# The forgetting attention goes first, with the other attention's preparation laid between its units

## The reference

```
proj = u @ w_in                      # c_q 256, c_kv 128, k_pe 32, fox q/k/v 3*512, f_logit 8
q = rms_norm(rms_norm(c_q) @ w_uq)   # MLA: 8 heads of 96; the last 32 rotated by position
kv = rms_norm(c_kv) @ w_ukv          # 64 key numbers and 64 values a head
k = rms_norm(concat(k_nope, k_pe))   # k_pe is the same 32 numbers for all heads; rotated
o_mla = attention(q, k, v, 96 ** -0.5)
fq, fk = rms_norm(fox_q), rms_norm(fox_k)           # FoX: 8 heads of 64
cum = cumsum(log_sigmoid(f_logit + b_forget))
o_fox = attention(fq, fk, fv, 64 ** -0.5, cum)      # adds cum[t] - cum[s] to the scores
return concat(o_mla, o_fox) @ w_out
```

## Time and profile before

| | |
|---|---|
| median of 3 runs (lowest, highest) | 1681.85 us (1679.6, 1686.58) |
| profiled execution, its own time | 1693.18 us |
| its span, first to last instruction | 1691.4 us |
| mean granted TensorE clock | 0.949 |
| busy: TensorE, VectorE, ScalarE, GpSimd | 91%, 61%, 32%, 33% |
| chain that ended last | TensorE 69%, DMA 20%, VectorE 6%, ScalarE 2% |
| DMA, mean over the span | 338 GB/s |

### The profile page before, as it was taken

How to read it: one execution, slowest core, us unless ns; L and a number is a source line. 1 busy time by engine, 2 the same in 40 slices (tenths; PEclk the granted TensorE clock), 3 DMA queues, 4 the chain that set the end, 5 groups by cost and what they waited for, 6 DMA issues and landing times.

```text
span 1691.4 us, 22760 instructions
## 1 busy us (share of the span) xinstructions
PE 1530.7 (91%) x8260; PEld 1172.0 (69%) x8260; DVE 1024.1 (61%) x2113; ACT 534.0 (32%) x1077; POOL 558.2 (33%) x361
## 2 busy tenths in 40 slices
PE   6999989999999999999999998978887778688877
PEld 6999988678899999998889986534433333233332
DVE  4554355555343325998974845757676776758556
ACT  4433353343344435443115422212121212121213
POOL 3555344000144342001001413444544445353441
PEclk9999999799899998998999999999998989898999
DMA  6767699977889997998976828899999999999995
GB/s 247 254 225 253 235 348 386 322 249 261 299 314 367 371 371 276 363 368 303 324 260 237 321 81 370 321 426 426 427 427 427 427 427 428 426 427 427 427 427 248
DMA packets 98724, 571.87 MB, mean 338 GB/s; under 512 B 10960, under 2 KB 11088, under 8 KB 48976
## 3 DMA queue, kind: packets, MB, share of 16 engines
q1 hardware_dynamic: 60768, 298.41, 48.5%
q0 software_dynamic: 36864, 268.45, 37.8%
q10 hardware_dynamic: 1008, 3.90, 0.6%
HBM read 569.68 MB, written 135.27 MB: 417 GB/s over the span
## 4 chain that ended last, share of the span: by engine, by line
PE 69%; DMA 20%; DVE 6%; issue 2%; ACT 2%; POOL 1%; another core or an unknown queue 0%; ACTq 0%; POOLq 0%; DVEq 0%
DMA arena<-pairs,eidx 18%; PE ps L2213 10%; PE ps L1669 9%; PE ps L1670 9%; PE ps L1671 9%; PE ps L2014 5%; PE ps L2183 2%; PE ps L1720 2%; PE ps L1722 2%; PE ps L1721 2%; DMA ring<-pairs,eidx 2%; PE ps L2031 2%; PE ps L1965 2%; DVE arena L1565 1%; PE ps L1684 1%
## 5 line engine op out<-in xcount | busy, mean ns | idle before, releaser
L2213 PE MATMUL ps<-arena 128*128 128x512 f32 x872 | 420.6, 634 | 90.2 <-ACT arena L1025 90.1
L2213 PEld LDWEIGHTS ps<-arena 128*128 128x128 f32 x872 | 173.0, 203 | 324.6 <-issue 201.9
L1565 DVE CUSTOM_DVE_ANT_0 arena<-arena 128x1024 f32<-128x1024 f32 x218 | 265.4, 1223 | 166.1 <-DMA arena<-pairs,eidx 165.9
L654 POOL TENSOR_TENSOR w_lo<-ring,w_hi 128x1024 fp32r<-128x1024 f32 x82 | 219.0, 2672 | 430.0 <-DVE w_lo L1095 350.3
L684 POOL DMA_INDIRECT arena<-pairs,eidx x218 | 253.6, 1163 | 297.9 <-PE ps L2213 240.1
L1669 PE MATMUL ps<-u_hi,w_hi 128*128 128x256 f32 (+1 forms) x1056 | 305.9, 290 | 10.9 <-DVE u_lo L1064 10.9
L1671 PE MATMUL ps<-u_hi,w_lo 128*128 128x256 f32 (+1 forms) x1056 | 304.2, 288 | 0.0
L1670 PE MATMUL ps<-u_lo,w_hi 128*128 128x256 f32 (+1 forms) x1056 | 303.9, 288 | 0.0
L701 ACT ACTIVATE w_hi<-ring 128x1024 fp32r<-128x1024 f32 x188 | 198.0, 1056 | 170.4 <-PE ps L1722 77.5
L1669 PEld LDWEIGHTS ps<-u_hi,w_hi 128*128 128x128 f32 x1056 | 202.7, 192 | 13.1 <-issue 11.7
L1671 PEld LDWEIGHTS ps<-u_hi,w_lo 128*128 128x128 f32 x1056 | 203.2, 192 | 0.0
(11 more groups left out here) (305 smaller groups left out, 2329.1 us busy)
## 6 DMA issues: line engine op xcount, KB each, us to landing
ring<-in_stream SPq DMA_DIRECT2D x130, 1024.0 KB, 6.7
pairs<-in_peer_u SPq DMA_DIRECT2D x128, 512.0 KB, 7.4
pairs<-in_peer_v SPq DMA_DIRECT2D x128, 512.0 KB, 8.5
arena<-in_ada SPq DMA_DIRECT2D x32, 768.0 KB, 6.3
arena<-pairs,eidx POOLq DMA_INDIRECT x218, 17.2
h<-in_x_t SPq DMA_DIRECT2D x1, 1088.0 KB, 7.4
arena<-in_keys ACTq DMA_DIRECT2D x1, 1024.0 KB, 6.4
out<-arena SPq DMA_DIRECT2D x2, 512.0 KB, 5.2
```

Of the source, the lines that this page charges most:

```text
L654: pool.tensor_tensor(lo[:, half, :], ring[:, slot, e * HALF:(e + 1) * HALF], hi[:, half, :], ALU.subtract).then_inc(used if e else lo_done, 1)
L1565: dve.tensor_tensor_reduce(row, row, hf[:, n % HEAD_ROWS // TOPK, :], 1.0, 0.0, ALU.mult, ALU.add, dots[:, n % HEAD_ROWS:n % HEAD_ROWS + 1 ...
L2213: mm = pe.matmul(ps[:, Y_BANKS[j // TOPK] + half, :], diag[:, n % DIAGS, :], slot_of(n)[:, D + half * 512:D + half * 512 + 512], start=(hd ...
```

## The change

FoX's units get the numbers 0 to 15, MLA's 16 to 31 (`head_of`). Stage 3 is cut up and laid into iterations of the FoX units; all its products go through one bank (7), the squares through bank 2, so that FoX's scores have two banks instead of three. In the FoX loop TensorE turns unit n first, then computes the scores of n+2. A preparation product waits until the bank is read. The turned probabilities get a buffer of their own. The key part that all heads share is rotated once, from one copy, and then copied to the eight heads. The forget gate's Exp and Ln go ahead of the raw keys' evictions. The preparation by iteration:

| iteration | TensorE | VectorE | ScalarE |
|---|---|---|---|
| 0 to 3 | query rotation; 16 squares (0, 1 queries; 2, 3 keys) | three `rope` operations | |
| 4 | shared key's rotation; last squares | rotation, copy to eight heads | |
| 5 to 7 | values of a token tile | 7: inverses of the roots | 6: roots; 7 to 9: value copies |
| 8 to 15 | spread of a key's scale | product with it | |

```diff
@@ scalar
+            act.wait_ge(z_done, 3)
+            act.activation(logf[fr, 1, :], logf[fr, 1, :], ACT.Exp, scale=-1.0).then_inc(f_exp, 1)
+            act.wait_ge(f_exp, 1)
+            act.activation(logf[fr, 2, :], logf[fr, 1, :], ACT.Ln, bias=1.0).then_inc(f_ln, 1)
             for hd in range(HEADS):
                 act.wait_ge(k_raw_mm, hd + 1)
...
                 if n >= 3:
                     head_out(n - 3)
+                if n == ROOT_AT:
+                    key_roots()
+                if ROOT_AT < n <= ROOT_AT + 3:
+                    values(n - ROOT_AT - 1)
@@ vector
-            dve.tensor_scalar(km[pr, :, :], pe_all, V("g_k")[pr], None, ALU.mult).then_inc(kpe_done, 1)
+            dve.tensor_scalar(km[pr, 0, :], praw[pr, 3, :], V("g_k")[pr], None, ALU.mult).then_inc(kpe_done, 1)
...
+            def key_turned():
+
+                shared = pe_sq[pr, :]
+                dve.wait_ge(krot_mm, 1)
+                dve.wait_ge(rope_step, 12)
+                dve.tensor_tensor(turned[pr, 0, :], ps[pr, SPARE_BANK, 0:T], C("sin")[pr, :], ALU.mult).then_inc(rope_step, 1)
+                dve.tensor_tensor(shared, km[pr, 0, :], C("cos")[pr, :], ALU.mult).then_inc(rope_step, 1)
+                dve.wait_ge(rope_step, 14)
+                dve.tensor_tensor(shared, shared, turned[pr, 0, :], ALU.add).then_inc(rope_step, 1)
+                dve.wait_ge(rope_step, 15)
+                dve.tensor_copy(km[pr, :, :], shared[:, None, :].broadcast_to([ROPE, HEADS, T])).then_inc(rope_step, 1)
...
             for n in range(units):
                 if n + 1 < units:
                     soft_max(n + 1)
                 scale_p(n)
+                if n < 4:
+                    query_turned(n)
+                elif n == 4:
+                    key_turned()
+                elif n == ROOT_AT + 1:
+                    key_scales()
+                if KEYS_FROM <= n < KEYS_FROM + HEADS:
+                    key_scaled(n - KEYS_FROM)
                 if n % 2 and n >= units // 2:
                     ada_add(KT // 2 + n // 8, n // 2 % ADA_Q)
@@ tensor
             pe.wait_ge(fstat_sqrt, 2)
+            pe.wait_ge(q_raw_ev, 4)
+            pe.wait_ge(k_raw_ev, HEADS)
             pe.wait_ge(kpe_done, 2)
+            pe.wait_ge(fox_done, 12)
...
+            def values_of(t):
+
+                at, n = token_tiles(0, 3)[t]
+                if t:
+                    pe.wait_ge(vm_ev, t)
+                else:
+                    pe.wait_ge(rope_step, 13)
+                pe.matmul(ps[0:n, SPARE_BANK, :], ckvn[:, at:at + n], wuv, start=True, stop=True).then_inc(vm_mm, 1)
...
             def key_norm(hd):
 
-                if hd >= 4:
-                    pe.wait_ge(kn_done, hd - 3)
+                if hd:
+                    pe.wait_ge(kn_done, hd)
+                else:
+                    pe.wait_ge(mrec2, 1)
+                    pe.wait_ge(vm_ev, 3)
...
             def scores_of(n):
...
-                if n >= 3:
+                if n > FOX_UNITS:
                     pe.wait_ge(exp_done, n - 2)
+                elif n == FOX_UNITS:
+                    pe.wait_ge(mstat_sqrt, 2)
+                elif n >= 2:
+                    pe.wait_ge(exp_done, n - 1)
...
             scores_of(0)
             scores_of(1)
-            for n in range(units):
+            for n in range(FOX_UNITS):
+                turn_probs(n)
+                scores_of(n + 2)
+                if n < 4:
+                    query_rotated(n)
+                elif n == 4:
+                    key_rotated()
+                if n < TT:
+                    query_squares(n)
+                elif n < TT + 3:
+                    key_squares(n - TT)
+                if VALUES_FROM <= n < VALUES_FROM + 3:
+                    values_of(n - VALUES_FROM)
+                if KEYS_FROM <= n < KEYS_FROM + HEADS:
+                    key_norm(n - KEYS_FROM)
+                if n:
+                    weigh(n - 1)
+            for n in range(FOX_UNITS, units):
                 if n + 2 < units:
                     scores_of(n + 2)
                 turn_probs(n)
-                if n:
-                    weigh(n - 1)
+                weigh(n - 1)
```

More of the change, by code:

```diff
@@ L528, in w_parts, with head_of, score_bank @@
             return (late_hi, late_lo, late_hi_f) if part == 2 else (w_hi, w_lo, w_hi_f)
+        UNITS = 2 * HEADS * TT
+        FOX_UNITS = HEADS * TT
+        VALUES_FROM = 5
+        ROOT_AT = 6
+        KEYS_FROM = 8
+        SPARE_BANK = 7
+        STAT_BANK = 2
+        def head_of(n):
+            return (n // TT + HEADS) % (2 * HEADS)
+        def score_bank(n):
+            return n % 2 if n < FOX_UNITS else (n - FOX_UNITS + 2) % 3
         def q_scale(hd, t):
@@ L820, in _, with key_roots, values @@
                 act.activation(ksq[0:NOPE, hd, :], src, ACT.Square).then_inc(k_raw_ev, 1)
[L821 to L826, removed]
-                n = P if t < 2 else N_META
-                act.activation(vM[0:n, t, :], ps[0:n, t, :], ACT.Copy).then_inc(vm_ev, 1)
-            fr = slice(FL_ROW, FL_ROW + HEADS)
-            act.wait_ge(z_done, 3)
-            act.activation(logf[fr, 1, :], logf[fr, 1, :], ACT.Exp, scale=-1.0).then_inc(f_exp, 1)
-            act.wait_ge(f_exp, 1)
-            act.activation(logf[fr, 2, :], logf[fr, 1, :], ACT.Ln, bias=1.0).then_inc(f_ln, 1)
-            units = 2 * HEADS * TT
+            def key_roots():
+                act.wait_ge(mstat_mm, 1)
+                act.activation(mrms[:, 0:32], ps[:, STAT_BANK, 0:32], ACT.Sqrt, bias=eps[:, :]).then_inc(mstat_sqrt, 1)
+                act.activation(mrms[0:N_META, 32:40], ps[0:N_META, STAT_BANK, 32:40], ACT.Sqrt, bias=eps[0:N_META, :]
+                               ).then_inc(mstat_sqrt, 1)
+            def values(t):
+                n = P if t < 2 else N_META
+                act.wait_ge(vm_mm, t + 1)
+                act.activation(vM[0:n, t, :], ps[0:n, SPARE_BANK, :], ACT.Copy).then_inc(vm_ev, 1)
+            units = UNITS
             for n in range(units):
-                hd, t = divmod(n, TT)
+                hd, t = head_of(n), n % TT
                 keys_n = X0 + P * (t + 1)
@@ L1211, in rope, with query_turned @@
                 dve.tensor_tensor(x, x, tmp, ALU.add).then_inc(rope_step, 1)
-            for b in range(4):
+            def query_turned(b):
                 dve.wait_ge(qrot_mm, b + 1)
-                rope(qm[0:QK, 2 * b:2 * b + 2, :], ps[0:QK, HEAD_BANKS[b], :].rearrange("p (a t) -> p a t", a=2),
+                rope(qm[0:QK, 2 * b:2 * b + 2, :], ps[0:QK, SPARE_BANK, :].rearrange("p (a t) -> p a t", a=2),
                      slice(X0, T), b)
[L1217 to L1224, removed]
@@ L1849, in _ @@
                 mla_key(4 + j)
[L1851 to L1859, removed]
@@ new lines, in key_rotated, with query_squares, key_squares @@
+            def key_rotated():
+                pe.wait_ge(rope_step, 10)
+                pe.matmul(ps[0:QK, SPARE_BANK, 0:T], C("rot")[0:QK, 0:QK], km[0:QK, 0, :], start=True, stop=True).then_inc(krot_mm, 1)
+            def query_squares(s):
+                at, n = token_tiles(0, 2)[s]
+                for hd in range(HEADS):
+                    pe.matmul(ps[0:n, STAT_BANK, s * 8 + hd:s * 8 + hd + 1], qsq[0:QK, hd, at:at + n], one, start=True, stop=True)
+            def key_squares(s):
+                at, n = token_tiles(0, 3)[s]
@@ L1891, in _ @@
-            mm.then_inc(vm_mm, 1)
-            for hd in range(4, HEADS):
-                key_rotated(hd)
-            pe.wait_ge(mrec2, 1)
-            pe.wait_ge(vm_ev, 3)
-            for hd in range(HEADS):
-                key_norm(hd)
-            pe.wait_ge(kn_done, HEADS)
-            units = 2 * HEADS * TT
+            units = UNITS
             def scores_of(n):
-                hd, t = divmod(n, TT)
+                hd, t = head_of(n), n % TT
                 keys_n = X0 + P * (t + 1)
```

58 lines of the change are left out of this document (32 added, 26 removed).

## The result

The changed kernel took 1706.98 us (median of six, 1697.39 to 1717.84), the kernel before 1684.21 beside it (1678.82 to 1692.83); the ratio is 1.0116, with a 95% interval of 1.0086 to 1.0147. On the median of 1681.85 known before that is +19.5 us, to 1701. The profiled execution took 1708.26 us against 1693.18.

The account below looks back on a forecast made before the run. Units looked close to TensorE's own work; laid-in preparation would close a TensorE-VectorE ring. Stage end 5.9 us later plus 4 us of clock loss gave +9.9 us on the 1681.85 median: 1692 us, range 1677 to 1703.

Parts of the forecast that it names:

- the first two mechanisms: FoX units: a ring of waits between TensorE and VectorE, and one short clock loss, +4 us.
- the clock's 4 us: Units 0 to 4: one rotation unit at half clock, +4 us, within bounds of 0 and 20.
- Start: Before the first unit: forget gate ahead of ScalarE's key evictions, first scores at 310.5 us, first turning at 314.6.
- The ring: FoX units: turning, scores, product, VectorE's preparation and unit work follow one another; 73.2 us against TensorE's own 60.3.
- The clock in units 0 to 4: Squares and idling in FoX units 0 to 4 put one unit at half clock, +4 us.
- The table loads: ScalarE's function switches inside the units: 1.28 us each; the skill's drain, 2.8 us more for two, was left out.
- The MLA units: Last sixteen units: ada additions cost nearly nothing; seventh 25.2 us after the first instead of 23.4, stage end at 421.4.
- the credit of two full buffers: MLA units: first two ada pieces already loaded, offsetting DMA steps of 5.0 us against 3.9 us of units.
- the ada pieces don't keep up at all: Rival, MLA units: they run at 5 us, +5 on the forecast, 1697 us; inside the forecast's range, no separate chance.
- the rival of a lasting clock loss: Units 0 to 4: clock falls early and stays low through the squares, about 1701 us; chance 0.15.
- The first rival, TensorE's own work: New units: TensorE's work bounds them, VectorE runs ahead; stage ends 8.8 us earlier, 1673 us; chance 0.1.
- nothing is left of the seven rotations: Key preparation: one shared rotation stands for eight; seven removed, TensorE 0.55 us and VectorE 1.3 us each.

Follow-up runs that it names:

- e2: Changed kernel with VectorE's preparation of each iteration done one iteration later, behind the scaling of the next unit; ratio to the kernel before 1.0040.
- e1: Changed kernel with all 32 blocks of table rows paired ahead of the ada pieces instead of 24; ratio to the kernel before 1.0099.
- e11: Changed kernel with VectorE's preparation one iteration later and SyncE's last eight blocks behind all eight ada pieces; ratio to the kernel before 1.0037.
- e3: Changed kernel with two unused 256-column products in each eight one-column squares of units 0 to 4; ratio to the kernel before 1.0104.
- e5: Changed kernel with VectorE's preparation one iteration later and all 32 blocks ahead of the ada pieces; ratio to the kernel before 1.0141.
- e8: Changed kernel with VectorE's preparation one iteration later and SyncE's last eight blocks behind the first two ada pieces; ratio to the kernel before 1.0077.
- e9: e8's kernel with two unused 256-column products in each eight squares of units 0 to 4; ratio to the kernel before 1.0098.
- e10b: Kernel before with the shared key part rotated once and two unused 256-column products behind the value products; median 1682.41 us, ratio to the kernel before 0.9975.
- e7: Kernel before with only the shared key part rotated once, in the old place, e4's edit again; ratio to the kernel before 0.9981.
- e4: Kernel before with only the shared key part rotated once, in the old place, and copied to eight heads; ratio to the kernel before 1.0002.

## Why the prediction was wrong

The direction and the first two mechanisms held; the size didn't: +19.5 us against the +10 foretold. The range ended at 1703, 4 us below the 1707 measured (by the ratio, on the median known before, it is 1701). With the clock's 4 us the sum put the projection at 425.4, and it started at 435.25: of these 9.9 us the start has 1.7, the sixteen FoX units 0.3 and the MLA units 7.9.

*Start.* Foretold: first scores 310.5, turning 0 at 314.6. Measured 312.36 and 316.28. The last query's eviction was already 1.4 us late there, ahead of all that was changed; the rest, 0.3 us up to turning 0, is mine. The last link before the first scores was VectorE's running sum (311.16 to 312.23) and not ScalarE's evictions, which I had counted.

*The ring.* Foretold 5.45 for unit 0, 3.75 and 4.65 in the later ones. Measured 5.23, 3.50 and 4.31, TensorE waiting for VectorE as described, and e2 took it away by changing only VectorE's order. My rounds were 0.2 to 0.3 us too long, no more.

*The clock in units 0 to 4.* Foretold one unit at half clock, +4 us. It fell in every one of units 1 to 4. Turning 0 to 5 was 35.5 us, where the ring alone gives 29.2: +6.3. The shorter ring behind made up for it, so turning 16 came 77.5 us after turning 0, against a forecast of 77.2 with the clock's share. That these agree is luck: one term was 2.3 us short, the rest 2.0 us long.

*The table loads.* The row of ScalarE in unit 6 answers to the earlier trace rows:

```profile
352.42 1.28 ACT L846 ACT_TABLE_LOAD   x1
353.71 0.29 ACT L846 ACTIVATE arena<-ps,eps 128x32 f32<-128x32 f32 x1
353.90 0.24 ACT L847 ACTIVATE arena<-ps,eps 16x8 f32<-16x8 f32 x1
354.16 1.28 ACT L863 ACT_TABLE_LOAD   x1
```

A load begins 0.02 us behind a copy's end and the root 0.01 us behind the load's. The 1.38 us drain that the Trainium skill ("ScalarE: Activation LUTs", "What ACT_TABLE_LOAD costs") adds to each load isn't there, as it wasn't before; keeping the row was right.

*The MLA units: the step that failed.* "The seventh addition comes 25.2 us after the first instead of 23.4", and so 33.6 us from turning 16 to the projection. It was 29.7 us (394.72 to 424.40) and 41.5. I had summed the DMA work and seen that it is longer than the units, but I let the credit of two full buffers absorb it without a stop. The fifth addition was due 16.6 us behind the first by the units' pace (16.5 in e1). My 25.2 is five steps of 5.04 us from bytes over peak rate, and three such steps put the fifth piece at 15.1, in time. It came at 18.5: between the steps the engines weren't full (shares of 0.81 and 0.83 at 398 and 402), and the piece could only be issued when the third addition had freed its buffer, at 405.0, and took 8.2 us from issue to landing behind the block in front of it. So VectorE stood for 2.0 us, TensorE with it, the clock fell at 416 and stayed down to 440. Of the 7.9 us that the term was short, 2.7 are the waits themselves, the rest is the half clock; the projection adds 1.1 (41.7 us to the next feed-forward instead of 40.6). e1 and e11, which have no late piece, put the stretch at 32.7 and 32.9 us: 33.6 was right for units without a stop. That the additions themselves cost nothing was nearly right too: some 1.5 us (e1). In all nine profiles of the changed kernel and its variants the clock fell in the MLA units where additions waited (the changed kernel twice, e2, e3, e5, e8, e9) and held at 1.00 where none did (e1, e11).

I had this as a rival ("the ada pieces don't keep up at all"), but priced it at 5 us, the pace of the DMA, and not at what a stop does to the clock. And the rival of a lasting clock loss was placed in units 0 to 4 alone. The first rival, TensorE's own work, is refuted for the order as written, and e2 and e11 show what it was worth once VectorE's order allows it: projections at 418.3 and 411.7 us. That nothing is left of the seven rotations was right in the changed kernel; in the old place their absence is worth about 4 us (e10b), or 5 us at the projection (e7).

What stays open: why the clock fell in e2's MLA units behind two waits of 1.0 us, and in e3's only behind the fifth of five (0.2 to 1.1 us); and how much of e1's 8.8 us in the stage reaches the whole time, which its ratio is too wide to say.

## What to carry to other kernels

Work laid into another loop's idle time lengthens the loop if the engine that does it stands between two links of the chain: compare the sum along the chain, not the busy shares, and let the laid-in piece follow the unit's own work by one turn. When units get shorter, whatever feeds them by a queue must be checked for the first, the middle and the last item, with landing times instead of rates; a late item costs its wait and then what TensorE's clock loses. Before a dense run of small products, see in the profile that the clock is up, and in more than one execution; a wide product in an idle gap there can be worth more than the work it adds.

## What wasn't expected of the hardware

A half clock can outlast a full load. TensorE counted busy for 41.90 of 41.90 us (e4) and 20.00 of 20.00 (e5) in MLA units, and the granted clock stayed at 0.50. Of the 147 instructions of that stretch of e4, 121 are products of 128 columns, 12 of 144 and 14 of 272. It came back 2.8 us behind the start of the first FoX scores in e4 (6 of the 13 instructions there have 144 columns, the others 128), and 2.9 to 5.8 us into the projection, whose products have 256 columns, in the seven profiles where it had fallen behind late additions. The Trainium skill ("TensorE: Matmul & The Clock Gate", Part 1) says that sustained activity releases the throttle; here time counted as busy was not enough.

The same stretch can have another clock in the next execution: units 0 to 4 with the ring open had 0.87, 0.79, 1.00 and 0.87 (e2, e5, e8, e11), 22.7 to 27.9 us. Two 256-column products in a gap, 1.1 us, stand between six executions of twelve near 1710 us (e7; four of twelve in e4) and none of twelve (e10b), each of the three on another chip.
